# Where the Hyena filters are computed: both in expert passes 2 to 6 instead of at the head of each layer, with seven ring positions from the second lap on and the layer loop written out

## The chip, the cores and the metric

One Trainium2 chip, one core, float32 throughout. The time of a run is device microseconds of that core; fewer is better. The chip writes a float32 product as two matmul rows, so a count of matmul rows is twice the number of products in the code.

## The reference

Two blocks follow each other on x (256 tokens, 1024 features). The first has an mLSTM/gMLP mixer, a cross attention and a mixture of 32 experts. The second has two layers, each with three branches (Hyena convolution, gated linear attention, pooling), gates, and a feed-forward part. What the change touches is the Hyena filter, which depends on weights and positions alone and not on x:

```python
def _hyena_filter(t, z, w1, b1, fr1, w2, b2, fr2, w3):
    h = jnp.sin(fr1 * (z @ w1 + b1))
    h = jnp.sin(fr2 * (h @ w2 + b2))
    h = (h @ w3).astype(jnp.float32)
...
    decay = jnp.exp(-t * jnp.abs(deltas))
    h_fwd = h[:, :D_HYENA] * decay
    h_bwd = h[:, D_HYENA:] * decay
    return jnp.concatenate([h_fwd, zero, h_bwd[:0:-1]], axis=0)

def _hyena_mixer(u, conv_w, conv_b, t, z, w1, b1, fr1, w2, b2, fr2, w3, bias):
...
    k = _hyena_filter(t, z, w1, b1, fr1, w2, b2, fr2, w3)
    Zf = jnp.fft.rfft(zv, n=2 * L, axis=1)
    Kf = jnp.fft.rfft(k, n=2 * L, axis=0)
    y = jnp.fft.irfft(Zf * Kf[None], n=2 * L, axis=1)[:, :L]
...
    for i in range(DEPTH_2):
        h = _rms_norm(x, norm_mix_pre[i])
        proj = h @ w_in[i]
```

The transforms are products with cosine and sine tables.

## The kernel before

Each engine has its own program, written by hand, and runs the same list of regions in order: `first` (mixer, attention, routing), eight expert passes `pass0` to `pass7`, `extra` (a loop whose trip count is read on the chip: experts with more than 32 tokens get their further tokens here; with these inputs it runs once), `between` (final norm of the first block), `layers` (a hardware loop of two trips) and `last`. Engines meet on semaphores only. `Place.need` works out the count to wait for; inside the hardware loop it's a register's value plus a constant.

**Weights.** SP loads 2 MB blocks into ring positions: ten exist (`spots`), four as tensors of their own, six inside `zone`, where positions 0, 5, 6 and 9 also lie under tables and tiles of the layers. An expert pass computes four experts at once (32 tokens of each, side by side in the PE's columns) from 12 blocks: four for gate, four for up, four for down. Block k of all 96 goes to position k mod 10. `load` in `sp_prog` waits until the position's last user is done and issues the DMA. On PE, `slot` waits for the block; `release` only notes the position, and `first_mm` puts the signal `w_used` on the first product that comes behind and isn't alone in its group, or `flush` gives it at the end of the pass. The layers use a ring of four positions [7, 8, 3, 4] for 37 blocks a layer.

**A pass on PE** (`expert_pass`): tokens gathered by products (in0, in1), weights transposed, gate and up products, then `hid` transposed, down products, and products that scatter the result back (out). ACT and DVE evacuate between them. Blocks 0 to 9 are loaded ahead of pass 0.

**The head of a layer on PE** (`pe_layer`): transposes of the normed x (`norm_T`), f1 (filter, first product), hy0 (a block of the input projection, 32 products), f2, hy1, f3 (four products), hy2, then the four k groups (the filter's transform, ten products), then `lr`, q, gk, kk, zt and so on. DVE (`dve_layer`) takes each sine's argument to within pi in six instructions (`sine`), runs the three-tap convolutions of hy (`hconv`), multiplies f3 by the decay and forms sum and difference (hp_, hm_). ACT does the sines, the copies into `pad3`, and the copies of k into `Kf`. `zv`, the product of two convolved parts, is needed by the zt transposes behind kk.

**`between` on SP** waits for positions 0, 6 and 9 and loads the filter's weights, vec2, the whole table (2.9 MB), small2 and gate2 for layer 0; ACT loads the next layer's at each layer's end. `extra` loads three blocks into positions 1, 2 and 5, each when its position's last user is done.

Of the kernel before, what the change touches and what calls it, by code (L numbers as in the profile page):

```python
# [42 lines left out]
ZONE = 35200  # L43
# [11 lines left out]
EXPERT_RING = list(range(SPOTS))  # L55
EXTRA_RING = [1, 2, 5]
LAYER_RING = [7, 8, 3, 4]
PASS = [f"pass{i}" for i in range(PASSES)]

# [19 lines left out]
def _columns(table, parts):  # L79
    at = 0  # L80
    for name, n in parts:
# [14 lines left out]
_columns(TABLE, [("dft", 1024), ("sin0", 256), ("nyq", 128), ("inv", 1024), ("decay", 1024), ("band", 2048),  # L96
                 ("zT", 256)])
# [49 lines left out]
class Book:  # L147


    def __init__(self, counts):  # L150
        self.order = ["first"] + PASS + ["extra", "between", "layers", "last"]

        self.trips = {r: 1 for r in self.order} | {"extra": 0, "layers": NL}
# [7 lines left out]
class Banks:  # L161
# [46 lines left out]
    def all_taken(self, pl):  # L208
# [5 lines left out]
COUNTS = {'between': {'hs': 2,  # L214
             'ld_filt': 16,
             'ld_gate2': 16,
             'ld_small2': 16,
             'ld_table': 16,
             'ld_vec2': 16,
             'ms': 3,  # L220
             'pads': 1,
             'pool_step': 1,
             'rstd': 3,
             'sq': 4,
             'x_done': 2},
# [48 lines left out]
           'ld_const': 16,  # L274
           'ld_ident': 16,
# [3 lines left out]
           'ld_vec1': 16,  # L279
           'ld_x0': 16,  # L280
# [36 lines left out]
 'layers': {'Osq': 1,  # L317
# [5 lines left out]
            'filled0': 16,  # L323
            'filled1': 16,
            'filled2': 16,
            'filled3': 16,
            'filled4': 16,
            'filled5': 16,
            'filled6': 16,
            'filled7': 15,  # L330
            'filter': 1,
# [7 lines left out]
            'ld_filt': 16,  # L339
# [3 lines left out]
            'ld_vec2': 16,  # L343
# [6 lines left out]
            'sin': 2,  # L350
            'sinarg': 2,
            'sq': 12,
            'taken0': 16,
            'taken1': 16,
            'taken2': 16,
            'taken3': 16,
            'taken4': 16,
            'taken5': 16,
            'taken6': 16,
            'taken7': 15,  # L360
            'vector_step': 140,
# [12 lines left out]
            'zv': 1},  # L374
 'pass0': {'filled0': 2,
# [6 lines left out]
           'filled7': 1,  # L382
           'placed': 1,
# [9 lines left out]
           'w_ready0': 32,  # L393
           'w_ready1': 32,
           'w_ready2': 16,
# [7 lines left out]
           'w_used0': 2,  # L403
           'w_used1': 2,
           'w_used2': 1,
# [32 lines left out]
           'w_ready6': 16,  # L438
           'w_ready7': 16,
           'w_ready8': 16,  # L440
           'w_ready9': 16,
           'w_used0': 1,
           'w_used1': 1,
           'w_used2': 2,
# [2252 lines left out]
```

## Time and profile before

| what | value |
|---|---|
| runs (3) | 1986.69, 1986.70, 1989.63 us; median 1986.7 |
| profiled execution | 1987.02 us, its span 1984.8 us |
| mean granted TensorE clock | 0.932 of full |
| PE busy | 1754.0 us (88%), 7768 matmul rows |
| DVE, ACT, POOL busy | 467.6, 266.8, 23.4 us |
| DMA moved | 405.12 MB, mean 204 GB/s |
| first | 0 to about 330 us |
| passes 0 to 7 | about 330 to 770 us |
| extra and between | about 770 to 808 us |
| layer 0, layer 1 | 808 to 1391, 1391 to 1985 us |

Times of rows are us from the span's start. A busy share is an average over stages, so each stage is to be read by itself: which engine or transfer the others wait for there. "Idle before <-X" names what ended the wait; "issue" is a wait for nothing that the profile shows.

### The profile page before, as it was taken

How to read it: one execution, taken by the hardware profiler on the slowest of the kernel's cores; microseconds unless marked ns; L12 is line 12 of the kernel's file. 1: busy time of each engine (PE TensorE's matmuls, PEld its weight loads, DVE VectorE, ACT ScalarE, POOL GpSimd, SP SyncE). 2: the span in 40 equal slices, each digit the busy share in tenths (PEclk: the TensorE clock that was granted, in tenths of full speed). 3: DMA queues.
4: the chain of work that ended last, by engine and by line, in shares of the span. 5: the costliest groups of instructions: out<-in, count | busy, mean ns of one | idle time of the engine just before them, and what ended most of it. 6: DMA issues, size and time to landing. Idle time of an engine off the chain costs nothing.

```text
span 1984.8 us, 18851 instructions
## 1 busy us (share of the span) xinstructions
PE 1754.0 (88%) x7768; PEld 1164.0 (59%) x7768; DVE 467.6 (24%) x1005; ACT 266.8 (13%) x564; POOL 23.4 (1%) x46
## 2 busy tenths in 40 slices
PE   8999996766766667899999989999899999989998
PEld 7475654222221223676788568864676788578853
DVE  4223113311100111424321222211424322222211
ACT  2222121000000000213210010100113210010001
POOL 0010000000000000000000000000000000000000
PEclk9989997888777887899999989999899999989999
DMA  7432635999999999332233323361533133333260
GB/s 313 162 127 85 254 127 235 427 427 428 429 428 427 428 428 377 159 120 93 85 127 149 127 106 149 128 229 33 209 120 117 54 139 137 132 149 122 107 250 21
DMA packets 31781, 405.12 MB, mean 204 GB/s; under 512 B 3553, under 2 KB 4065, under 8 KB 7377
## 3 DMA queue, kind: packets, MB, share of 16 engines
q1 hardware_dynamic: 30608, 400.12, 50.2%
q10 hardware_dynamic: 1088, 3.78, 0.6%
q8 instruction: 64, 1.05, 0.2%
q14 instruction: 21, 0.16, 0.0%
HBM read 402.84 MB, written 1.05 MB: 203 GB/s over the span
## 4 chain that ended last, share of the span: by engine, by line
issue 60%; PE 22%; DMA 15%; DVE 2%; POOL 1%; ACT 1%; DVEq 0%; POOLq 0%; SPq 0%; ACTq 0%
PE bank L1016 22%; DMA zone<-in_w_experts 8%; DMA w<-in_w_experts 6%; PE bank L1060 1%; POOL stat L2547 1%; DVE zone L1890 0%; DMA x<-in_x 0%; DVE zone L1533 0%; DVE x L1940 0%; DVE zone L1773 0%; ACT zone L1356 0%; ACT zone L1348 0%; ACT zone L1374 0%; DVE x L1557 0%; DVE zone L1547 0%
## 5 line engine op out<-in xcount | busy, mean ns | idle before, releaser
L1016 PE MATMUL bank<-zone,w 128*128 128x256 f32 x3712 | 821.0, 384 | 4.4 <-DVE zone L1547 4.4
L1016 PEld LDWEIGHTS bank<-zone,w 128*128 128x128 f32 x3712 | 714.8, 193 | 112.2 <-issue 13.0
L1016 PE MATMUL bank<-w,zone 128*128 128x512 f32 (+1 forms) x1536 | 498.1, 659 | 64.5 <-DMA w<-in_w_experts 49.5
L1016 PE MATMUL bank<-zone 128*32 128x512 f32 (+9 forms) x2184 | 385.0, 532 | 89.4 <-DMA zone<-in_w_experts 62.4
L1016 PEld LDWEIGHTS bank<-w,zone 128*128 128x128 f32 (+1 forms) x1536 | 196.8, 164 | 347.6 <-issue 272.0
L1016 PEld LDWEIGHTS bank<-zone 128*128 128x128 f32 (+3 forms) x2184 | 205.2, 166 | 263.8 <-issue 154.6
L1374 ACT ACTIVATE zone<-bank 128x512 f32<-128x512 f32 (+2 forms) x136 | 77.5, 578 | 785.3 <-PE bank L1016 620.8
L1060 PE MATMUL bank<-const,zone 128*128 128x128 f32 (+2 forms) x286 | 47.6, 315 | 55.0 <-DVE zone L1533 34.5
L2341 DVE TENSOR_SCALAR zone<-zone,vec 128x256 f32<-128x256 f32 x68 | 28.0, 412 | 267.5 <-ACT zone L2199 267.5
L1060 PEld LDWEIGHTS bank<-const,zone 128*128 128x128 f32 (+2 forms) x286 | 38.3, 163 | 75.4 <-issue 30.7
L2199 ACT ACTIVATE zone<-bank 128x256 f32<-128x256 f32 x68 | 24.9, 384 | 360.0 <-PE bank L1016 360.0
L1888 DVE TENSOR_TENSOR zone<-zone,bank 128x512 f32<-128x512 f32 x8 | 5.5, 688 | 197.0 <-PE bank L1016 197.0
L2295 ACT ACTIVATE zone<-bank 128x512 f32<-128x512 f32 x16 | 9.6, 598 | 265.6 <-PE bank L1016 265.6
L2511 DVE TENSOR_TENSOR stat<-stat 128x1 f32<-128x1 f32 x8 | 1.3, 160 | 184.1 <-ACT zone L2295 184.1
L2547 POOL TENSOR_TENSOR stat<-stat 128x1 f32<-128x1 f32 (+2 forms) x29 | 17.3, 598 | 1924.4 <-DVE stat L1526 1924.4
L1890 DVE COPY zone<-bank 128x512 f32<-128x512 f32 x8 | 5.5, 692 | 143.3 <-PE bank L1016 143.3
L2494 DVE SCALAR_TENSOR_TENSOR zone<-zone,bank 128x256 f32<-128x256 f32 x16 | 6.8, 422 | 116.9 <-PE bank L1016 116.9
L2343 DVE SCALAR_TENSOR_TENSOR zone<-zone,vec 128x256 f32<-128x256 f32 x68 | 33.0, 485 | 2.4
L2342 DVE SCALAR_TENSOR_TENSOR zone<-zone,vec 128x256 f32<-128x256 f32 x68 | 33.0, 485 | 2.5
L1898 DVE TENSOR_TENSOR x<-bank,x 128x512 f32<-128x512 f32 x36 | 24.9, 692 | 17.7 <-PE bank L1016 17.7
L2476 DVE TENSOR_SCALAR zone<-bank 128x512 f32<-128x512 f32 x4 | 2.8, 692 | 79.3 <-PE bank L1016 79.3
L1016 PE MATMUL bank<-zone,const 4*128 4x256 f32 (+2 forms) x34 | 13.1, 550 | 8.6 <-DVE zone L1818 8.6
(228 smaller groups left out, 526.0 us busy)
## 6 DMA issues: line engine op xcount, KB each, us to landing
w<-in_w_layers SPq DMA_DIRECT2D x68, 2048.0 KB, 8.4
zone<-in_w_experts SPq DMA_DIRECT2D x61, 2048.0 KB, 42.1
w<-in_w_experts SPq DMA_DIRECT2D x38, 2048.0 KB, 42.1
w<-in_w_first SPq DMA_DIRECT2D x16, 2048.0 KB, 8.0
w<-in_w_layers SPq DMA_DIRECT2D x6, 1024.0 KB, 5.2
zone<-in_table SPq DMA_DIRECT2D x1, 2880.0 KB, 16.0
zone<-in_row ACTq DMA_DIRECT2D x2, 1024.0 KB, 4.8
const<-in_const SPq DMA_DIRECT2D x1, 1153.0 KB, 13.6
```

The source lines that it names most:

```text
L1016: return eng.matmul(out, lhsT, rhs, start=start, stop=stop, **kw_)
L1060: ins = eng.transpose(bank[0:m, at:at + n], src, idn)
L1374: A(dst, src, func, **k).then_inc(*banks.done(pl, name))
L1888: V.tensor_tensor(hid, sG, banks.tile(pl, "up"), ALU.mult).then_inc(*banks.done(pl, "up"))
L1898: V.tensor_tensor(xs, banks.tile(pl, f"out{t}{n}"), xs, ALU.add).then_inc(*banks.done(pl, f"out{t}{n}"))
L2199: return A(pad3[:, c % 3, 1:T + 1], bank[:, half * T:half * T + T], ACT.Copy)
L2295: A(ot[:, t, 512 * n:512 * n + 512], banks.tile(pl, name(t, n)), ACT.Square, accum_out=ssq[:, 4 + 2 * t + n:5 + 2 * t + n]).then_inc(*pl.u ...
L2341: v(pl, V.tensor_scalar(dst, src[:, 0:T], pv(VEC2, wname, 3 * c), pv(VEC2, bname, c), ALU.mult, ALU.add))
L2342: v(pl, V.scalar_tensor_tensor(dst, src[:, 1:T + 1], pv(VEC2, wname, 3 * c + 1), dst, ALU.mult, ALU.add))
L2343: V.scalar_tensor_tensor(dst, src[:, 2:T + 2], pv(VEC2, wname, 3 * c + 2), dst, ALU.mult, ALU.add).then_inc(*pl.up(signal))
L2494: w(V.scalar_tensor_tensor(m0, gates[:, c, :], 1.0, ba[:, 0:T], ALU.add, ALU.mult))
L2547: eng.tensor_tensor(rstd[:, col:col + n], ms[:, col:col + n], mhalf[:, 0:n], ALU.pow).then_inc(*pl.up(sem("rstd")))
```

## The change

It does five things. (1) f1, f2, f3 and k of both layers are computed in passes 2 to 6, between the up products and `hid`: f1 in pass 2, f2 in pass 3, f3 of layer 1 in pass 4, k of layer 1 and f3 of layer 0 in pass 5, k of layer 0 in pass 6. ACT's copies of k become DVE's. The results (`Kf`) stay in places of their own until the layers. (2) For tiles of the filter and for the first part of the table, positions 0, 5 and 6 are given up after their first use: from block 10 on the ring is [1, 2, 3, 4, 7, 8, 9]. (3) Loads move: the table is put in another order and its first 2432 of 5760 columns are loaded behind pass 0's blocks, with the filter's third matrices (64 partitions, 256 KB each); vec2 and the small filter matrices of both layers come in `first`; the rest of the table stays in `between`. (4) The layer loop is written out, and its waits are for constants. (5) The ring of the layers runs on from layer 0 to layer 1, where it began anew.

```diff
-EXPERT_RING = list(range(SPOTS))
+LATER_RING = [1, 2, 3, 4, 7, 8, 9]
+EXPERT_RING = list(range(SPOTS)) + [LATER_RING[i % len(LATER_RING)] for i in range(PASSES * ESLOTS - SPOTS)]
...
+        def filters(pl):
+            if pl.region == "pass2":
+                eng.wait_ge(*pl.need(sem("ld_filt"), 0))
+                eng.wait_ge(*pl.need(sem("ld_ftable"), 0))
+                for i in range(NL):
+                    group(pl, f"f1{i}", [((HFO, 0, T), [(w1f[i], tv("zT", HEMB))])])
+            elif pl.region == "pass3":
+                for i in range(NL):
+                    eng.wait_ge(*pl.need(sem("sin"), i + 1 - NL))
+                    group(pl, f"f2{i}", [((HFO, 0, T), [(w2f[i], h12[i])])])
+            elif pl.region == "pass4":
+                eng.wait_ge(*pl.need(sem("ld_filt3"), 0))
+                eng.wait_ge(*pl.need(sem("sin"), 0))
+                filter_out(pl, 1)
+            elif pl.region == "pass5":
+                eng.wait_ge(*pl.need(sem("filter"), 0))
+                filter_dft(pl, 1)
+                filter_out(pl, 0)
+            elif pl.region == "pass6":
+                eng.wait_ge(*pl.need(sem("filter"), 0))
+                filter_dft(pl, 0)
...
                 ins.then_inc(*banks.close(pl, kind))
+            filters(pl)
             for evacuated in banks.taken_up(pl, "up"):
...
-        group(pl, "f1", [((P, 0, T), [(w1f, tv("zT", HEMB))])])
...
-        tall(pl, "hy0", hT, 4)
-        eng.wait_ge(*pl.need(sem("sin"), 1))
-        group(pl, "f2", [((P, 0, T), [(w2f, h12)])])
-        tall(pl, "hy1", hT, 4)
-        eng.wait_ge(*pl.need(sem("sin"), 2))
-        for r in range(2):
-            for t in range(TT):
-                group(pl, f"f3{r}{t}", [((P, 0, 512), [(h12b[:, t * P:(t + 1) * P], w3f[:, 512 * r:512 * r + 512])])])
-        tall(pl, "hy2", hT, 4)
...
+        for i in range(3):
+            tall(pl, f"hy{i}", hT, 4)
...
+            eng.wait_ge(*pl.need(sem("w_used0"), 1))
+            eng.dma_start(table[:, 0:FILTER_TABLE], dram["table"][:, 0:FILTER_TABLE]).then_inc(*pl.up(sem("ld_ftable"), 16))
+            eng.wait_ge(*pl.need(sem("w_used6"), 1))
+            for layer in range(NL):
+                eng.dma_start(w3f[layer], dram["w_filt3"][layer]).then_inc(*pl.up(sem("ld_filt3"), 16))
...
         def between(pl):
-            for at in (0, 6, 9):
-                eng.wait_ge(*pl.need(sem(f"w_used{at}"), 0))
-            eng.dma_start(filt, dram["w_filt"][0]).then_inc(*pl.up(sem("ld_filt"), 16))
-            eng.dma_start(vec2, dram["vec2"][0]).then_inc(*pl.up(sem("ld_vec2"), 16))
-            eng.dma_start(table, dram["table"]).then_inc(*pl.up(sem("ld_table"), 16))
+            eng.wait_ge(*pl.need(sem("sin"), 0))
+            eng.wait_ge(*pl.need(sem("w_used9"), 0))
             eng.dma_start(small2, dram["w_small2"][0]).then_inc(*pl.up(sem("ld_small2"), 16))
             eng.dma_start(gate2, dram["w_gate2"][0]).then_inc(*pl.up(sem("ld_gate2"), 16))
+            eng.dma_start(table[:, FILTER_TABLE:], dram["table"][:, FILTER_TABLE:]).then_inc(*pl.up(sem("ld_table"), 16))
...
-                with eng.Fori(0, book.trips[region]) as it:
-                    parts[region](Place(book, region, it))
+                parts[region](Place(book, region))
```

On DVE the filter's steps (`sine`, `filter_sides`, `filter_kept`, the last with four copies of 128x512) stand behind the product of `hid` and ahead of the copy of down1; on ACT the sines of passes 2 and 3 stand between the copies of `hid` and of down0.

The head of a layer on PE. Before, from f3 to `lr` (16x256); bank<-zone,w 128x256 are the hy products, x10 the k groups, REGISTER_ALU the counts of the loop's waits:

```order
L1016 MATMUL bank<-zone 128x512 x2
L1045 REGISTER_ALU
L1016 MATMUL bank<-zone 128x512 x2
L1023 REGISTER_ALU
L1016 MATMUL bank<-zone,w 128x256 x16
L1045 REGISTER_ALU
L1016 MATMUL bank<-zone,w 128x256 x16
L2019 REGISTER_ALU
L1045 REGISTER_ALU
L1016 MATMUL bank<-zone 128x512 x10
L1045 REGISTER_ALU
L1016 MATMUL bank<-zone 16x256 x16
```

Of the change, from the transposes on, in either layer:

```order
L1069 MATMUL bank<-const,zone 128x128 x16
L1025 MATMUL bank<-zone,w 128x256 x96
L1025 MATMUL bank<-zone 16x256 x16
L1025 MATMUL bank<-zone,w 128x256 x32
L1025 MATMUL bank<-zone 128x256 x8
```

The three hy blocks (96 products) now stand together, `lr` right behind them.

Pass 5 on PE, from its last gate and up blocks to the next pass's gathers. Before (32x512 are expert products, 128x128 x4 the transposes of `hid`, 128x512 x4 out):

```order
L1016 MATMUL bank<-w,zone 32x512 x16
L1016 MATMUL bank<-zone 32x512 x16
L1016 MATMUL bank<-w,zone 32x512 x8
L1060 MATMUL bank<-const,zone 128x128 x4
L1016 MATMUL bank<-w,zone 32x512 x8
L1016 MATMUL bank<-zone 32x512 x24
L1016 MATMUL bank<-zone 128x512 x4
L1016 MATMUL bank<-zone 128x128 x16
```

Of the change:

```order
L1025 MATMUL bank<-w,zone 32x512 x32
L1025 MATMUL bank<-zone 32x512 x24
L1025 MATMUL bank<-zone 128x512 x14
L1069 MATMUL bank<-const,zone 128x128 x4
L1025 MATMUL bank<-w,zone 32x512 x32
L1025 MATMUL bank<-zone 128x512 x4
L1025 MATMUL bank<-zone 128x128 x16
```

Fourteen products of the filter (ten of k, four of f3) stand between up and `hid`.

SP at the end of pass 0. Before:

```order
L2588 DMA zone<-in_w_experts 128x4096 x2
L2588 DMA w<-in_w_experts 128x4096 x2
L2588 DMA zone<-in_w_experts 128x4096 x4
L2588 DMA w<-in_w_experts 128x4096 x2
L2588 DMA zone<-in_w_experts 128x4096 x2
```

Of the change:

```order
L2641 DMA w<-in_w_experts 128x4096 x2
L2641 DMA zone<-in_w_experts 128x4096 x3
L2689 DMA zone<-in_table 128x2432
L2692 DMA zone<-in_w_filt 64x1024 x2
L2641 DMA w<-in_w_experts 128x4096 x4
L2641 DMA zone<-in_w_experts 128x4096 x3
```

The part of the table and the two loads of filter weights go ahead of pass 1's first block.

## Rows read from the trace of the kernel before

**Rows 1.** The page's slices of 49.6 us each: DMA busy tenths, and GB/s.
```profile
DMA  7432635999999999332233323361533133333260
GB/s 313 162 127 85 254 127 235 427 427 428 429 428 427 428 428 377 159 120 93 85 127 149 127 106 149 128 229 33 209 120 117 54 139 137 132 149 122 107 250 21
```

**Rows 2.** Stretches of 20 us: busy us of each engine, PEclk, DMA share, GB/s.
```profile
440.00:460.00 20.00, 11.48 (x68) 2.57 (x68) 0.69 (x1) 0.60 (x1) 0.00 (x0) 0.83 1.00 424
1220.00:1240.00 20.00, 20.00 (x95) 17.60 (x94) 5.15 (x12) 2.06 (x6) 0.00 (x0) 1.00 0.31 130
```

**Rows 3.** PE timeline, passes 4 and 5: start, us, instruction, [idle before <-releaser].
```profile
583.17 3.64 PE L1016 MATMUL bank<-zone 128*32 128x512 f32 x16 [1.10 <-DMA zone<-in_w_experts]
...
596.72 5.36 PE L1016 MATMUL bank<-zone 128*32 128x512 f32 x48 [1.05 <-issue]
...
622.56 1.92 PE L1016 MATMUL bank<-w,zone 128*32 128x512 f32 x16 [1.38 <-DMA w<-in_w_experts]
...
627.55 3.17 PE L1016 MATMUL bank<-w,zone 128*32 128x512 f32 x16 [1.59 <-DMA w<-in_w_experts]
```

**Rows 4.** DMA issues, 330 to 770 us: count, KB, median us to landing.
```profile
zone<-in_w_experts SPq DMA_DIRECT2D x54, 2048.0 KB, 42.4
```

**Rows 5.** Five us at pass 0's start; columns as in rows 2.
```profile
330.00:335.00 5.00, 4.46 (x44) 1.76 (x48) 1.67 (x7) 0.00 (x0) 0.00 (x0) 1.00 0.21 46
```

**Rows 6.** PE's timeline, pass 0.
```profile
330.54 5.36 PE L1016 MATMUL bank<-zone 128*32 128x512 f32 x48 [1.12 <-issue]
...
342.55 1.93 PE L1016 MATMUL bank<-w,zone 128*32 128x512 f32 x16
```

**Rows 7.** DMA issues, whole span; columns as in rows 4.
```profile
w<-in_w_layers SPq DMA_DIRECT2D x68, 2048.0 KB, 8.4
...
zone<-in_table SPq DMA_DIRECT2D x1, 2880.0 KB, 16.0
```

**Rows 8.** PE's timeline, layer 0: hy1 and hy2, with f2 and f3 ahead.
```profile
824.60 0.70 PE L1016 MATMUL bank<-zone 64*128 64x256 f32 x2
825.23 14.08 PE L1016 MATMUL bank<-zone,w 128*128 128x256 f32 x64
839.24 3.70 PE L1016 MATMUL bank<-zone 64*128 64x512 f32 x8
842.87 14.08 PE L1016 MATMUL bank<-zone,w 128*128 128x256 f32 x64
```

**Rows 9.** PE by form, 808 to 870 us: count, busy us, mean ns, idle.
```profile
L1016 PE MATMUL bank<-zone 128*128 128x512 f32 x20 | 8.7, 592 | 0.0
```

**Rows 10.** PE's waits, 808 to 1400 us: us in total, times, longest.
```profile
PE bank L1016 <- DVE zone L2467: 0.2, 1, 0.2
```

**Rows 11.** Timeline from the leftover pass to layer 0's first product.
```profile
760.05 3.64 PE L1016 MATMUL bank<-zone 128*32 128x512 f32 x16 [1.25 <-DMA zone<-in_w_experts]
...
770.19 0.37 SPq L2640 DMA_DIRECT2D zone<-in_w_experts  x1
...
780.19 6.05 PE L1016 MATMUL bank<-zone 128*32 128x512 f32 x32
...
804.69 0.75 DVE L1533 TENSOR_SCALAR zone<-x,stat 128x1024 f32<-128x1024 f32 x1 [0.66 <-POOL stat L2547]
...
808.85 15.82 PE L1016 MATMUL bank<-zone,w 128*128 128x256 f32 x64
```

**Rows 12.** Timeline from layer 0's last products to layer 1's first.
```profile
1369.51 16.47 PE L1016 MATMUL bank<-w,zone 128*128 128x512 f32 x38
...
1391.39 3.05 PE L1060 MATMUL bank<-const,zone 128*128 128x128 f32 x12 [5.41 <-issue]
...
1392.52 0.75 DVE L1533 TENSOR_SCALAR zone<-x,stat 128x1024 f32<-128x1024 f32 x1 [0.66 <-POOL stat L2547]
...
1397.24 1.12 PE L1060 MATMUL bank<-const,zone 128*128 128x128 f32 x4 [2.80 <-issue]
...
1400.46 16.95 PE L1016 MATMUL bank<-zone,w 128*128 128x256 f32 x64 [0.96 <-DVE zone L1547]
```

More of the change, by code:

```diff
@@ L58 @@
 PASS = [f"pass{i}" for i in range(PASSES)]
+LAYER = [f"layer{i}" for i in range(NL)]
 def spot(ring, k, first=0):
@@ L150, in __init__ @@
     def __init__(self, counts):
-        self.order = ["first"] + PASS + ["extra", "between", "layers", "last"]
-        self.trips = {r: 1 for r in self.order} | {"extra": 0, "layers": NL}
+        self.order = ["first"] + PASS + ["extra", "between"] + LAYER + ["last"]
+        self.trips = {r: 1 for r in self.order} | {"extra": 0}
         self.counts = {r: counts.get(r, {}) for r in self.order}
@@ L1318, in extra, with layer @@
             eng.wait_ge(*pl.need(sem("extra_added"), 1))
-        run(eng, dict(first=first, extra=extra, layers=lambda pl: pe_layer(
-            pl, eng, group, transposes, norm_T, tall, wide, widest, slot, release, flush, mm, first_mm)) | {r: expert_pass for r in PASS})
+        def layer(pl):
+            pe_layer(pl, eng, group, transposes, norm_T, tall, wide, widest, slot, release, flush, mm, first_mm)
+        run(eng, dict(first=first, extra=extra) | {r: expert_pass for r in PASS} | {r: layer for r in LAYER})
     def run(eng, parts):
@@ L1510, in between, with layer @@
                 A(hs[:, t, :], x[:, t, :], ACT.Square, accum_out=ssq[:, t:t + 1]).then_inc(*pl.up(sem("sq")))
-        run(eng, dict(first=first, extra=extra, between=between,
-                      layers=lambda pl: act_layer(pl, eng, A, evac_T, copy, load_small2)) | {r: expert_pass for r in PASS})
+        def layer(pl):
+            act_layer(pl, eng, A, evac_T, copy, load_small2)
+        run(eng, dict(first=first, extra=extra, between=between) | {r: expert_pass for r in PASS} | {r: layer for r in LAYER})
     g8, e8, em, pen = lg[:, 80:96], lg[:, 96:112], lg[:, 112:176], lg[:, 176:184]
@@ L1942, in between, with layer @@
             scale_rows(pl, x, 4)
-        run(eng, dict(first=first, extra=extra, between=between,
-                      layers=lambda pl: dve_layer(pl, eng, V, v, ms_of, scale_tile, evac_T)) | {r: expert_pass for r in PASS})
+        def layer(pl):
+            dve_layer(pl, eng, V, v, ms_of, scale_tile, evac_T)
+        run(eng, dict(first=first, extra=extra, between=between) | {r: expert_pass for r in PASS} | {r: layer for r in LAYER})
     z = Zone(area, area + 4 * SLOT)
@@ L2573, in between, with layer @@
                 pw(pl, 2 + t, t, 1)
-        def layers(pl):
+        def layer(pl):
             for k in range(2 * TT * 2):
                 pw(pl, k + 1, (4 if k % 2 == 0 else 0) + k // 2 % TT, 1)
-        run(eng, dict(first=first, between=between, layers=layers))
+        run(eng, dict(first=first, between=between) | {r: layer for r in LAYER})
     def sp_prog(eng):
@@ L2660, in last @@
             eng.wait_ge(*pl.need(sem("stored"), 16))
[L2662 to L2667 removed]
+        run(eng, dict(first=first, extra=extra, between=between, last=last) | {r: expert_pass for r in PASS} | {r: layer for r in LAYER})
     with nc.Block() as block:
```

707 lines of the change are left out of this document (364 added, 343 removed).

## The prediction

> **What bounds the kernel now.** I read the page's slices first. From 350 to 750 us the DMA engines are full at 427 to 429 GB/s [rows 1]; before and behind they move a third of that. The 20 us tables say who works: from 440 to 460 us PE is busy 11.5 of 20 us at a mean granted clock of 0.83, with the DMA share at 1.00; from 1220 to 1240 us PE is busy all 20 us at clock 1.00 (2.4 GHz), with the DMA share at 0.31 [rows 2]. So there are two regimes: the expert passes are paid in bytes, the two layers in PE instructions. Then I read PE's timeline in a pass: PE waits for each block, and the last up block begins at 622.56 us, 39.39 us and eight blocks behind the last down block of the pass before: 4.92 us a block [rows 3], which is 2.1 MB at 427 GB/s. In the layers I read PE's timeline and its list of waits.
>
> **The filter's work in the layers (removed).** The chip writes a float32 product as two matmul rows. In layer 0, f2 holds PE from 824.60 to 825.23 (0.63 us), f3 from 839.24 to 842.87 (3.63 us) [rows 8], and the four k groups are 20 rows, 8.7 us [rows 9], of which the pipelining overlaps 0.1: 8.6 us. f1 stands before hy0, and hy0, at 808.85, waits for DVE's copy of the transposed norm anyway; f1 is hidden there and its removal gives nothing. Sum 12.86 us a layer, with no idle time of PE between the pieces, and 25.7 us for two. Does this reach the end? Between hy0 and the merging PE's list has one wait on another engine, 0.2 us on DVE [rows 10]. Everything that DVE and ACT do for later products (gates, decays, Y) hangs on products behind `lr`, and comes forward with them. The convolutions are fed by the hy products, 3.5 us of PE a chunk for three DVE instructions; only zv is older than `lr`, and it's needed behind q, gk and kk. DVE's six-step sines, its sums and ACT's copies and sines go too, all beside PE: 0 us. What is late next is nothing new: PE's own products. **-25.7 us.**
>
> **The written-out loop (moved).** At the turn from layer 0 to layer 1 PE ends its products at 1369.51 + 16.47 = 1385.98 us. The rows of token tile 0 have long been ready, but its transposes start only at 1391.39, after 5.41 us laid to "issue"; the last four of tile 1 stand again 2.80 us on "issue", and hy0 starts at 1400.46 [rows 12], 7.19 us behind the end of tile 1's scaling (1392.52 + 0.75). At the entry to layer 0, with no jump back, the same distance is 808.85 - (804.69 + 0.75) = 3.41 us [rows 11]. So 3.8 us of the turn belong to the jump. hy0 itself takes 16.95 us there and 15.82 at the entry, against 14.08 for a warm block [rows 8, 11, 12]: PE stood longer before it, and the clock came later; 1.1 us more. Bounds: 0 (stalls stay) and the 8.2 us of both stalls. I take **-4.9 us**, by the entry's row. The Trainium skill (Runtime: NRT & Kernel Launch, Instruction fetch mechanics) says that fetching ahead is purely sequential and a taken branch outside a two-page window stalls; by it the stalls are the jump's, and the sum would stand. The register arithmetic before the loop's waits shows no price: DVE's wait for POOL takes 0.66 us at the entry, where the counts are constants, and 0.66 in the loop [rows 11, 12]. 0 us.
>
> **The filter's work in passes 2 to 6 (added).** PE gets 2 groups of f1, 2 of f2, f3 in pass 4, four k groups and f3 in pass 5 and four k groups in pass 6, each between the last up product and `hid`. The most is pass 5: 14 products, 28 rows of 0.43 us, 12 us. They lie in time that PE would spend waiting for down blocks: before, up ends at 624.5 and the first down block starts at 627.55; now it starts near 640, with three blocks landed, which PE takes in 1.9 us each against 4.92 for the DMA, so by the fourth it has caught up. `hid` is queued behind the filter on PE, and ACT's and DVE's copies of `hid` and down behind that, all inside this time. DVE's ten instructions in pass 5 stand ahead of the copy of down1, which is due some 20 us later. 0 us, with the cover being the DMA's own 19.7 us for four blocks; without cover it would be 12 us.
>
> **Seven positions (changed).** A block's position is freed by the first product of the next block. So six blocks, 29.5 us, are queued when PE takes a block on landing; before it was nine, and 42.4 us from issue to landing says the same [rows 4]. The longest pause in freeing is at a pass's end: 583.17 to 596.72, 13.6 us, 2.8 blocks [rows 3]. In pass 5 the pause before down grows to 17 us, 3.5 blocks. Three blocks of cover remain at the worst. 0 us; the upper bound is in the rivals.
>
> **Bytes brought into the full stretch.** 2432 of the table's 5760 columns, 1216 of 2880 KB [rows 7], 2.9 us at 427 GB/s; w3 twice 256 KB, 1.2 us. Both queue on SP behind pass 0's last blocks; w3 waits for position 6, whose user's successor starts at 342.55, and SP's later loads with it. By then blocks 10 and 11 and the table, 12.7 us of DMA from about 336 on, keep the queue full [rows 5, 6]. w3 goes to 64 partitions; the Trainium skill (SBUF — State Buffer, Door 1) says that 64 reach half of the ports. By it w3 would take 2.4 us and the sum be 1.2 us worse; no row here shows a 64-partition load alone. Without the rule I bound w3 by 0 and, at the 377 GB/s of the slice with the small loads [rows 1], 1.4.
>
> **The first lap's end.** Block 10 waited for block 0's position and now waits for block 1's: three blocks take PE 5.36 us [rows 6], so the DMA, idle to about 334 (share 0.21) [rows 5], starts 1.7 us later, and being full from there on it never makes this up. Together **+5.8 us** on the end of pass 7; lower bound 2.9 (the table alone), upper 7 (SP held by w3 for one more block's products).
>
> **The stage between.** The leftover pass's second weight block used to be issued when block 92 was used; now position 2 holds block 95, freed at the flush, so it goes with the third at 770.19. It has 13 us until its product, behind the gate product of 780.19 [rows 11]; two blocks take 9.8 and some 3 of latency (8.4 us from issue to landing alone [rows 7]). 0 us, bounded by 3. Behind it stand small2, gate2, 1664 KB of table and hy0's weights: 8.1 MB from 770, 19 us and 3 of latency, to 793, against hy0 at 808.85: 0 us. The first stage loads 0.24 MB more, beside products: 0 us.
>
> **Sum.** -25.7 - 4.9 + 5.8 = -24.8 us on the profiled execution's 1987.0 us (span 1984.8 and 2.2 around it): 1962.2. Its time is 0.3 above the median of the runs, 1986.7, so the forecast is **1962 us**. A measurement of this kernel tells about 0.2%, 4 us, from no change.
>
> **Rivals.**
> Stalls in the passes. If PE's granted clock stays at its lower level through pass 5's filter (after a wait it often is: the block at 622.56 takes 1.92 us, that at 627.55 3.17 [rows 3]), 28 rows take 24 us, the pause reaches 30 us and eats all 29.5 us of queue; 4.9 us to refill once or twice, 5 to 10 us: 1967 to 1972. Against it: after a pause the first block of products (15.82 for 14.08) loses only 1.7 us [rows 8, 11]. Chance 0.11.
> The turn's stalls stay. If an engine pays for first-run code whether it jumps or not, -4.9 becomes 0: 1967. The Trainium skill's rule above speaks against it, and layer 0's entry shows no such stall. Chance 0.08.
> The queue runs dry in every pass (slower). Seven positions leave the DMA without work at each pass's end, in seven passes. It decides from 3.5 us a pass, which eats the 24.8; at one block, 4.9 us, in passes 1 to 7 it is 34 us: 1996. For it: 42 us of queue became 29.5. Against it: the pauses are 13.6 and 17. Chance 0.03.
> An engine takes PE's place in the layers (DVE with the decays), and most of the 12.86 us a layer comes back as waits, with +5.8 paid: about 1983 to 1988, no change. Against it: rows 10. Chance 0.02.
>
> **How the numbers follow.** The forecast has 0.76; its own unknowns (the turn between the bounds, w3 and the start of the queue, the clock between the passes and layer 0, some 2 us either way) give 1957 to 1967. The range goes up to 1970, to hold the stalled turn and the milder half of the stalled passes, and from 1957. Faster by over 0.2%: 0.76 + 0.11 + 0.08 = 0.95; within 0.2%: 0.02; slower: 0.03.
>
> **What would show it.** Right: the last down block of pass 7 begins some 5.8 us later (760.05 before [rows 11]), with DMA at 427 GB/s through and block spacing still 4.92; PE in hy0 to lr without a gap, lr 12.9 us nearer to hy0; no "issue" wait at the turn and layer 1's hy0 some 10.7 us behind layer 0's last product. Wrong: a slice of the passes under 420 GB/s; PE waits for `taken`, `filter` or `sin`; new "issue" waits in layer 1's code, or one on DVE between lr and gates.

## The result, and the profile after

| | before | changed |
|---|---|---|
| median of the runs shown with it | 1987.0 us (4) | 1952.7 us (4: 1951.2 to 1953.4) |
| ratio, 95% interval | | 0.9823, 0.9806 to 0.9840 |
| profiled execution, its span | 1987.0, 1984.8 us | 1952.2, 1950.3 us |
| mean granted TensorE clock | 0.932 | 0.941 |
| PE busy, matmul rows | 1754.0 us, 7768 | 1731.3 us, 7768 |

The time fell by 34 us. The forecast was 1962 with a range from 1957 to 1970: the sign was right, and the gain was 9.5 us larger than the sum of 24.8. Beside the experiments the kernel before was run 49 times more, in three sets; their medians are 1984.2 (21 runs), 1984.3 (11) and 1985.9 us (17), and single runs lie between 1977.2 and 1990.2. So one profiled execution set against another, as in the table below, carries a part that isn't the change's.

From the page of the changed kernel: the rows that answer to [rows 1], and the chain that ended last (shares of the span by engine):

```profile
DMA  7432544999999999733233324352333142333260
GB/s 316 173 130 87 226 162 154 402 430 430 429 429 430 429 430 387 287 129 121 87 130 151 130 86 173 130 225 108 141 118 130 49 167 109 157 145 133 84 237 22
...
PE 76%; DMA 19%; DVE 2%; issue 1%; ACT 1%; POOL 0%; DVEq 0%; POOLq 0%; SPq 0%; ACTq 0%
```

The DMA is full through the passes, at 429 to 430 GB/s where it had been 427 to 429, with one slice at 402 where the added loads lie. PE's timeline in pass 5, start, us, instruction, idle before:

```profile
627.27 3.64 PE L1025 MATMUL bank<-zone 128*32 128x512 f32 x16 [1.72 <-DMA zone<-in_w_experts]
632.12 16.52 PE L1025 MATMUL bank<-zone 128*32 128x512 f32 x44 [1.21 <-DMA zone<-in_w_experts]
648.57 0.66 PE L1069 MATMUL bank<-const,zone 128*128 128x128 f32 x4
650.12 7.07 PE L1025 MATMUL bank<-w,zone 128*32 128x512 f32 x64 [0.89 <-ACT zone L1421]
658.04 3.67 PE L1025 MATMUL bank<-zone 128*128 128x512 f32 x8 [0.85 <-issue]
```

The 44 rows are the last up block (16) and the 28 rows of the filter. They end at 648.6; then all four down blocks are there and go in 7.07 us without a wait. The filter lies in time in which PE would have waited. PE behind pass 7, at layer 0's head, around `lo` and at the turn:

```profile
763.62 3.27 PE L1025 MATMUL bank<-zone 128*32 128x512 f32 x16 [1.91 <-DMA zone<-in_w_experts]
768.46 1.92 PE L1025 MATMUL bank<-zone 128*32 128x512 f32 x16 [1.58 <-DMA zone<-in_w_experts]
771.29 3.67 PE L1025 MATMUL bank<-zone 128*128 128x512 f32 x8 [0.90 <-DVE zone L2000]
778.23 5.41 PE L1025 MATMUL bank<-zone 128*128 128x32 f32 x32 [3.26 <-DVE zone L2019]
...
784.23 4.92 PE L1025 MATMUL bank<-zone 128*32 128x512 f32 x32
...
811.70 41.68 PE L1025 MATMUL bank<-zone,w 128*128 128x256 f32 x192 [1.09 <-DVE zone L1600]
853.31 7.08 PE L1025 MATMUL bank<-zone 128*16 128x256 f32 x32
...
1101.07 7.13 PE L1025 MATMUL bank<-w,zone 128*128 128x512 f32 x16 [1.82 <-DVE zone L2557]
1109.56 20.87 PE L1025 MATMUL bank<-w,zone 128*128 128x512 f32 x48 [1.35 <-DMA w<-in_w_layers]
...
1371.12 1.07 PE L1069 MATMUL bank<-const,zone 128*128 128x128 f32 x8 [0.38 <-issue]
1378.16 1.97 PE L1069 MATMUL bank<-const,zone 128*128 128x128 f32 x8 [5.97 <-DVE zone L1586]
1381.22 43.15 PE L1025 MATMUL bank<-zone,w 128*128 128x256 f32 x192 [1.09 <-DVE zone L1600]
1424.29 7.08 PE L1025 MATMUL bank<-zone 128*16 128x256 f32 x32
```

From `hy0` (811.70) to `lr` (853.31) PE runs 192 rows without a gap. At the turn the "issue" waits of [rows 12] are gone: tile 0's transposes come 0.38 us behind the last product, tile 1's wait for DVE's scaling, as at the entry. Stretch by stretch in us, from these rows and those ahead; one execution of each kernel:

| stretch | before | changed | difference | predicted |
|---|---|---|---|---|
| start to pass 0's first gate product | 330.5 | 332.1 | +1.6 | 0 |
| from there to pass 7's last down block | 429.5 | 436.3 | +6.8 | +5.8 |
| from there to layer 0's hy0 | 48.8 | 43.2 | -5.6 | 0 |
| hy0 to `lr`, layer 0 | 56.6 | 41.6 | -15.0 | -12.9 |
| `lr` to the last product, layer 0 | 520.6 | 517.4 | -3.2 | 0 |
| turn, last product to hy0 | 14.5 | 10.5 | -4.0 | -3.8 |
| hy0 to `lr`, layer 1 | 57.7 | 43.1 | -14.6 | -12.9, -1.1 |
| `lr` to the end of the span | 526.6 | 526.0 | -0.6 | 0 |

### The profile page after: what moved, and what is told of

It reads as the page before. It is cut to its first block, busy times and chain, and to the rows that moved or that the text cites. A ratio compares the mean times of both kernels' runs of the same rounds, so it can differ in the third digit from the quotient of the medians.

```text
span 1950.3 us, 17947 instructions
## 1 busy us (share of the span) xinstructions
PE 1731.3 (89%) x7768; PEld 1160.9 (60%) x7768; DVE 473.3 (24%) x1013; ACT 256.8 (13%) x552; POOL 23.5 (1%) x46
## 4 chain that ended last, share of the span: by engine, by line
PE 76%; DMA 19%; DVE 2%; issue 1%; ACT 1%; POOL 0%; DVEq 0%; POOLq 0%; SPq 0%; ACTq 0%
PE bank L1025 74%; DMA w<-in_w_experts 10%; DMA zone<-in_w_experts 9%; PE bank L1069 1%; DMA w<-in_w_layers 1%; POOL stat L2600 0%; DVE zone L1586 0%; DMA x<-in_x 0%; DVE zone L2568 0%; DVE x L2573 0%; ACT zone L1412 0%; DVE zone L1600 0%; ACT zone L2384 0%; ACT zone L2387 0%; DVE x L2050 0%
## 5 line engine op out<-in xcount | busy, mean ns | idle before, releaser
L1025 PE MATMUL bank<-w,zone 128*128 128x512 f32 (+1 forms) x1760 | 523.6, 653 | 75.7 <-DMA w<-in_w_experts 58.7
L1025 PEld LDWEIGHTS bank<-w,zone 128*128 128x128 f32 (+1 forms) x1760 | 203.8, 157 | 374.7 <-issue 287.5
L1025 PE MATMUL bank<-zone 128*32 128x512 f32 (+10 forms) x1960 | 339.3, 488 | 70.7 <-DMA zone<-in_w_experts 47.1
L1025 PEld LDWEIGHTS bank<-zone 128*128 128x128 f32 (+3 forms) x1960 | 194.7, 167 | 218.1 <-issue 132.4
L1421 ACT ACTIVATE zone<-bank 128x512 f32<-128x512 f32 (+1 forms) x128 | 72.7, 577 | 768.8 <-PE bank L1025 580.4
L1069 PE MATMUL bank<-const,zone 128*128 128x128 f32 (+2 forms) x286 | 46.9, 312 | 49.6 <-DVE zone L1586 41.0
L2295 ACT ACTIVATE zone<-bank 128x256 f32<-128x256 f32 x68 | 24.8, 384 | 358.6 <-PE bank L1025 358.6
(226 smaller groups left out, 526.6 us busy)
```

The costliest lines, as they stand in the source:

```text
L1025: return eng.matmul(out, lhsT, rhs, start=start, stop=stop, **kw_)
L1069: ins = eng.transpose(bank[0:m, at:at + n], src, idn)
L1421: A(dst, src, func, **k).then_inc(*banks.done(pl, name))
L2295: return A(pad3[:, c % 3, 1:T + 1], bank[:, half * T:half * T + T], ACT.Copy)
```

## Experiments

Twelve kernels ran. Each diff shows only the lines that carry the edit. The changed kernel itself has the four runs above and one profile; where a number here is set against its 1952.7 us, the runs come from different sets, whose medians of the kernel before lie within 1.8 us of each other. Where a stretch is counted from the "first transfer", that is the moment in pass 0 at which the DMA, idle till then, begins again, taken from windows of 1 us (334.5 us in before, 337.5 in the changed kernel), so good to some 0.3 us.

**1. The loop alone.**

```diff
-        self.order = ["first"] + PASS + ["extra", "between", "layers", "last"]
+        self.order = ["first"] + PASS + ["extra", "between"] + LAYER + ["last"]
```

> The kernel before with the layer loop alone written out (filters stay at the head of each layer, ten positions, the layers' ring begins anew in layer 1). Nothing ahead of 808.85 us (layer 0's hy0) may move. By the prediction's step: the turn from layer 0's last product (1385.98) to layer 1's hy0 (1400.46) falls from 14.5 to about 10.7 us, hy0 of layer 1 from 16.95 to 15.8: -4.9 us, 1982.1. Theory A (the extra gain of the change is the granted clock's, not the loop's): the same, between -4 and -5. Theory B (the register arithmetic ahead of the loop's waits has a price on the path): in addition some 1 to 1.5 us in each layer between lr and the last product, the wait of lo for its block shorter by 0.8 us in both: -6.5 to -8, 1979 to 1980.5.

Measured: 1973.3 us median (6), ratio 0.9953 (0.9935 to 0.9970), 6 to 13 us below before, where the prediction's step gave 4.9. PE's timeline of this kernel at the turn:

```profile
1375.86 1.07 PE L1119 MATMUL bank<-const,zone 128*128 128x128 f32 x8 [0.38 <-issue]
1382.90 1.97 PE L1119 MATMUL bank<-const,zone 128*128 128x128 f32 x8 [5.98 <-DVE zone L1592]
...
1385.96 6.38 PE L1075 MATMUL bank<-zone,w 128*128 128x256 f32 x20
```

Its DMA issues, columns as in [rows 4]:

```profile
w<-in_w_layers SPq DMA_DIRECT2D x68, 2048.0 KB, 7.7
```

The turn is 10.5 us, as in the change. In both layers the wait on DVE of [rows 10] is gone, the wait of `lo` for its block is 1.8 and 1.5 us (2.2 and 2.1 before), and a block lands 7.7 us behind its issue where it took 8.4 [rows 7]. Together these are some 1.2 us a layer that the prediction had at 0. But this kernel also differs ahead of 808.85, where nothing had been edited. PE at the head of layer 0:

```profile
803.78 14.05 PE L1075 MATMUL bank<-zone,w 128*128 128x256 f32 x64 [0.46 <-DVE zone L1606]
817.76 0.70 PE L1075 MATMUL bank<-zone 64*128 64x256 f32 x2
...
836.02 14.08 PE L1075 MATMUL bank<-zone,w 128*128 128x256 f32 x64
849.94 15.76 PE L1075 MATMUL bank<-zone 128*128 128x512 f32 x52
```

hy0 begins 5 us earlier and takes 14.05 for 15.82 us: the same instructions at another granted clock. With hy0 at the full clock, hy0 to `lr` is 849.94 + 8.7 - 803.78 = 54.8 us, against 41.6 without the filter: 13.2 us a layer.

**2. Seven positions alone.**

```diff
-EXPERT_RING = list(range(SPOTS))
+EXPERT_RING = list(range(SPOTS)) + [LATER_RING[i % len(LATER_RING)] for i in range(PASSES * ESLOTS - SPOTS)]
```

> The kernel before with seven ring positions from block 10 on, and nothing else. By the prediction: the last down block of pass 7 begins 1.7 us later (761.75 for 760.05), DMA at 427 GB/s through, no pause of DMA at any pass's end: 1988.7. Theory A (what PE's granted clock does at the end of pass 7 depends on where in time the blocks fall): the same 1.7 us, and then up to 5.5 us either way in the leftover pass: 1983 to 1990. Rival (seven positions starve the queue): each pass longer by up to 4.9 us, 2000 and more.

Measured: 1985.1 us (10), ratio 1.0016 (0.9996 to 1.0035). From pass 0's first gate product (333.17) to the last down block (764.50) 431.3 us, 1.8 more than before. DMA stays at 427.9 GB/s. The prediction's 1.7 holds, and the rival in which the queue runs dry is refuted.

**3 and 4. Without the filter's work, and also without its loads.** Both leave the filter's result out: the Hyena branch works with transforms set to zero.

```diff
-            filters(pl)
```
```diff
-            eng.dma_start(table[:, 0:FILTER_TABLE], dram["table"][:, 0:FILTER_TABLE]).then_inc(*pl.up(sem("ld_ftable"), 16))
-            eng.wait_ge(*pl.need(sem("w_used6"), 1))
-            for layer in range(NL):
-                eng.dma_start(w3f[layer], dram["w_filt3"][layer]).then_inc(*pl.up(sem("ld_filt3"), 16))
```

> The changed kernel without the filter's products, sines, sums and copies in passes 2 to 6 (the kept transforms are set to zero, so the Hyena branch's output is not computed from a filter; the loads stay). If the filter's work in the passes is wholly hidden, as the prediction has it, the last down block of pass 7 begins at 768.5 as in the changed kernel and the time is 1952.7 within 2 us. If it cost the passes anything: earlier by that, the prediction left 1.0 us of the passes unexplained. Theory C (the filter's products hold PE's granted clock up through the passes, and the 5.5 us between pass 7's last block and hy0 are theirs): without them this stretch is back at about 48.8 us, for 43.2, 1958.

> The changed kernel without the filter's work in the passes (the kept transforms are set to zero) and without the two loads behind pass 0's blocks (the table's first part, w3): the bytes brought into the full stretch, taken away alone. Runs so far, from pass 0's first gate product to pass 7's last down block: before 429.5 us, seven positions alone 431.3, change without filter work 436.4, the change 436.3. By the prediction's terms the bytes are 2.9 + 1.2 = 4.1 us: 432.3 here. By a load on 64 partitions at half speed 5.3: 431.1. Rival: the filter's or the loads' place in SP's queue (SP held by w3's wait) costs the rest: then above 431.3 by that. Time: about 5 us less than the change without filter work, 1947.

Measured: 1951.7 us (4) without the work, 1948.9 (6) without work and loads. Work: pass 0's gate to the last down block is 436.4 us against 436.3, so it is hidden, and theory C is refuted (pass 7's last block to hy0 is 46.3 us here, within what kernels with the filter's work show, 43.2 to 46.3). Loads: from the first transfer to the last down block 431.0 us with them, 423.5 without. That is 7.5 us for what was put at 4.1, and 423.5 is 2.1 less than the 425.6 of before. Two terms were off, in opposite directions. Stretches of 5 us of the changed kernel, columns as in [rows 2]:

```profile
350.00:355.00 5.00, 5.00 (x52) 1.73 (x44) 0.00 (x0) 0.29 (x1) 0.00 (x0) 1.00 1.11 270
355.00:360.00 5.00, 4.10 (x16) 1.44 (x8) 2.77 (x4) 0.30 (x1) 0.00 (x0) 1.00 0.96 343
```

The same of number 4, without the loads:

```profile
350.00:355.00 5.00, 5.00 (x52) 1.89 (x48) 0.00 (x0) 0.00 (x0) 0.00 (x0) 1.00 1.01 433
355.00:360.00 5.00, 4.11 (x22) 1.56 (x15) 1.81 (x3) 0.60 (x1) 0.00 (x0) 1.00 1.02 436
```

The DMA engines count as busy but move 270 and 343 GB/s where the small loads lie.

**5. Before, begun later.**

```diff
+            V.memset(kx.rearrange("p k t -> p (k t)"), 0.0)
+            V.memset(vx.rearrange("p t d -> p (t d)"), 0.0)
             scale_rows(pl, x, 2)
```

> The kernel before with two memsets of 128x2048 on DVE ahead of the first normalization, in tensors that are written later anyway: everything starts some 2 to 4 us later, no other work moves. Theory A (PE's granted clock after a wait depends on when in the run the wait falls): the delay d seen at the first product does not come out as 1987.0 + d, stretches behind waits (the gate rows near 136, the routing at 304 to 330, the stretch from pass 7's last block to hy0, 48.8 us) become longer or shorter by some tenths to 5 us, each without any change of work. Rival (the clock follows only from the order of work and waits, which is the same): each stretch as before within 0.3 us, and the time 1987.0 + d.

Measured: 1988.1 us (10), ratio 1.0007 (0.9990 to 1.0025). Pass 7's last block to hy0 took 46.5 us for 48.8, hy0 14.05 for 15.82, the turn 13.9 for 14.5. That speaks for theory A, but the 21 runs of the unchanged kernel beside it, spread over 13 us, say more: the clock that is granted behind a wait differs from one execution to the next. Over the profiled kernels this stretch took 48.8, 43.6, 45.2, 46.5 and 48.3 us with before's code (the last is number 9's), and 43.2, 46.3, 46.2, 46.3, 43.3 and 46.1 with the changed kernel's. Before's own profile was an unlucky one: the longest of its five.

**6. Each layer in a loop of one trip, and 7. the registers in its waits.**

```diff
+                with eng.Fori(0, 1) as it:
+                    parts[region](Place(book, region, it))
```
```diff
+                one = eng.value_load(xtab[0:1, 3 * XN:3 * XN + 1], min_val=0, max_val=XN)
+                parts[region](Place(book, region, one))
...
+            return sig.sem, (self.it + (base + n - 1) if base + n > 1 else base + n)
```

> The changed kernel with each layer in a hardware loop of one trip: the waits count by registers again (the arithmetic ahead of each wait is back), the code of either layer is still its own and no jump back is taken at the turn. Theory A (the registers' arithmetic is what the layers lost behind lr, 2.4 to 2.8 us a layer between the transposes of v's block and the last product; the jump is what the turn lost): both layers' stretches back from 477.2 and 476.7 to about 479 to 480, a wait of some 0.2 us on DVE in the gated attention, the waits at the merging and of lo longer by 0.1 and 0.3 to 0.7; the turn stays at 10.5 us: 1957. Rival 1 (the arithmetic is free, the layers' stretches follow the granted clock or the ring that runs on from layer to layer): no change, 1952.7. Rival 2 (it is entering a loop, not jumping back, that stalls the engines at the turn): the turn back to 14 us as well, 1960.

> The changed kernel, its layers still written out and without a loop, where every wait in them is for a register plus a constant, the register being a value read once per layer and engine (the count of the leftover pass's trips, 1 with these inputs). This puts the arithmetic ahead of the waits back, which a loop of one trip did not do. Theory A (the arithmetic is what the layers lost behind lr): the stretches from the transposes behind v's block's predecessor to the last product back from 477.2 and 476.7 to about 479, with a wait of 0.2 us on DVE in the gated attention and the DVE rows of the gates spaced by 0.19 for 0.10 us: about 1957. Rival (the loop's code, not its arithmetic, or the granted clock): stretches as they are within 0.5 us, 1952.7.

In number 6 the loop's counts came out as constants (DVE's steps in the gates stand 0.10 us apart, as in the change, not 0.19 as before), so it tested the loop's entry and exit alone: 1955.6 us (5), the turn at 10.5 us, the layers' stretches as in the change. No stall shows at the turn, where one loop ends and the next is entered. Its profiled span is 2.2 us longer, and the stretch behind pass 7 alone is 3.0 us longer (46.3 for 43.2), most of it in products at the lower clock. Yet its five runs (1954.5 to 1956.8) all lie above the changed kernel's four (1951.2 to 1953.4), so a cost of 1 to 3 us elsewhere isn't excluded. The Trainium skill (Runtime: NRT & Kernel Launch, Instruction fetch mechanics), which the prediction cited, says that a taken branch to outside the two fetched pages stalls, and the turn agrees: 13.9 to 14.5 us in the four kernels with the jump back, 10.5 without it. Number 7 has the arithmetic: 1953.2 us (5). DVE's timeline of number 7 in a gate shows its price:

```profile
1078.28 0.42 DVE L2560 TENSOR_TENSOR zone<-zone 128x256 f32<-128x256 f32 x1 [0.19 <-DVE zone L2556]
```

The stretches between the transposes behind `kk` and the last product are 477.4 and 476.8 us, against 477.2 and 476.7. Theory A is refuted: the arithmetic lengthens a dependent wait from 0.10 to 0.19 us and costs about 0.3 us a layer on PE's path, which shorter waits elsewhere cancel. The block's landing stays at 7.5 us with registers in SP's waits, and was 8.3 to 8.5 in each kernel with the loop of two trips, where the addresses come from a register as well. So the slower landing belongs to that loop; that the register address is its cause is a guess, which wasn't tried alone.

**8. w3 on 128 partitions.**

```diff
-    w3f = [spots[6][0:HFO, 2048:3072], spots[6][0:HFO, 3072:4096]]
+    w3f = [spots[6][:, 2048:2560], spots[6][:, 2560:3072]]
```

> The changed kernel with the filter's third matrices loaded on 128 partitions (two times 128x512, 256 KB as before) for 64 partitions of 1024; the second sine is also written to partitions 64 to 127, and f3's right half is taken from there. The runs show that the DMA moves 170 to 250 GB/s for 5 us where these loads lie, and that all bytes brought into the full stretch cost 7.5 us (431.0 from the first transfer to pass 7's last down block, 423.5 without them), of which the table's 1216 KB are 2.9. Theory D (the 64 partitions keep the DMA engines from sharing these loads evenly, 4.6 us for 512 KB): this stretch 427.7 to 428.5, no dip in GB/s, the time 3 us less, 1949.5. Rival (small loads cost that anyway, or SP's wait for position 6 does): 430.5 to 431, no change.

Measured: 1950.4 us (5: 1950.1 to 1952.8). From the first transfer to the last down block 427.6 us, 3.4 less (3.1 less if counted from pass 0's first gate product, 433.3 for 436.3), and the dip is gone. Its stretches of 5 us:

```profile
350.00:355.00 5.00, 4.14 (x40) 1.26 (x32) 0.69 (x1) 0.60 (x1) 0.00 (x0) 1.00 1.07 447
355.00:360.00 5.00, 4.70 (x17) 2.50 (x18) 2.76 (x4) 0.00 (x0) 0.00 (x0) 1.00 0.99 423
```

So two loads of 256 KB on 64 partitions cost 1.2 + 3.1 to 3.4, 4.3 to 4.6 us, in a full queue; numbers 3 and 4 give 7.5 - 2.9 = 4.6. The Trainium skill (SBUF — State Buffer, Door 1) says that 64 partitions reach half of the ports; the direction agrees, but the cost by it is an estimate of 2.4 us, which is less than the runs show. The edit also halves the bytes of a partition in each load, 4 KB to 2 KB, so what makes these loads so dear isn't separated.

**9. The address of the zone.**

```diff
+    sb("moved", VEC2["all"][1])
     zone = sb("zone", ZONE)
```

> The kernel before with an unused tensor of 173 columns ahead of the zone, so that the zone and the six ring positions in it begin at the byte address that they have in the changed kernel; nothing else is changed. DMA moves 427.8 GB/s from 362 to 755 us in the four runs with the old address and 430.0 in the five with the new one, and blocks into the zone come 4.84 us apart in place of 4.90. Theory E (the address of the ring's positions sets this): 430.0 GB/s, the last down block of pass 7 2.1 us nearer to the first transfer (423.5 for 425.7), the time 2 us less than before. Rival (it is the seven positions with the other order of places, or where the inputs lie in memory): 427.8 and no change.

Measured: 1983.9 us (12), ratio 0.9993 (0.9981 to 1.0005), so the time alone can't tell. The stretch can: from the first transfer to the last down block 423.3 for 425.6 us. The stretch from 400 to 740 us of before (columns as in [rows 2]):

```profile
400.00:740.00 340.00, 222.38 (x1376) 71.55 (x1376) 37.41 (x85) 17.00 (x41) 0.00 (x0) 0.83 1.01 428
```

The same of number 9:

```profile
400.00:740.00 340.00, 225.73 (x1384) 72.42 (x1376) 37.37 (x85) 17.01 (x41) 0.00 (x0) 0.83 1.01 431
```

An unused tensor of 692 bytes a partition ahead of the zone makes the weights' stream 0.6% faster. Number 9 has one profile, but the groups are clear: 428 GB/s in these 340 us in all four profiles with the old address, 430 or 431 in all with the new one. The change did this by accident, as vec2 became twice as wide and lies ahead of the zone.

**10, 11, 12. Products of constants in PE's waits.** They write a bank that is free and nobody reads; number 10 has them behind pass 7 and in the layers, number 11 in the first stage too, number 12 adds number 8's edit.

```diff
+            for i in range(n):
+                mm(banks.tiles[b], ident, const[:, 0:512], i == 0, i == n - 1)
```

> The changed kernel with products of constants (128x512, result never read) on PE where it waits: 3 behind pass 7, 8 ahead of layer 0's transposes, 6 between the two tiles' transposes at the turn, and 6 between those ahead of each feed-forward. They add 0.86 us each at the higher clock, all inside waits of 3.3, 9.0, 6.0 and 6.5 us, if the clock is at the higher level when they begin. Theory A (PE stands at the lower level behind a wait and pays for it, by luck of the run): the transposes behind the waits take 0.96 for 1.97 us (1.9 for 3.67 at layer 0's entry), layer 1's hy block 41.6 for 43.1, the leftover pass's gathers 3.8 for 5.4 and its gate and up 3.6 for 4.9, and the run to run spread shrinks: about 8 us less, 1944. Rival (these products do not hold the clock up, or they overrun the waits at the lower level): no change or up to 5 us more.

> The same, and in the first stage 4 products ahead of the transposes of the gate rows (wait of 3.9 us), 2 between the two tiles' transposes of two normalizations, 4 ahead of the ranks (wait of 8.6 us). Theory A: the stretch 136 to 150 shorter by 1 to 2 us, the block behind the second normalization 27.8 for 29.9, the gathers of pass 0 faster, pass 0's first gate product at about 328 for 332: 3 to 4 us below the kernel with the fillers behind pass 7 alone, 1941. Rival: the fillers begin at the lower clock and overrun, no gain or a loss of up to 3 us.

> The changed kernel with products of constants in PE's waits in the first stage, behind pass 7, at the head of the layers and ahead of the feed-forward, and the third matrices on 128 partitions. If the two gains (1952.7 to 1942.1 and about 3 us) are independent: 1939. If the fillers' gain was luck of the runs: 1946 to 1950.

Measured: 1945.7 (5), 1942.1 (6) and 1937.3 us (5), ratios to before 0.9808, 0.9788 and 0.9763 (0.9746 to 0.9779): number 12 beats both kernels, the changed one by 15 us, and the gains of 10 and of 2 to 3 us add. PE's timeline of number 10:

```profile
776.27 2.84 PE L1025 MATMUL bank<-const 128*128 128x512 f32 x6
779.43 3.76 PE L1025 MATMUL bank<-zone 128*128 128x32 f32 x32 [0.32 <-DVE zone L2034]
...
783.78 3.64 PE L1025 MATMUL bank<-zone 128*32 128x512 f32 x32 [0.34 <-DVE zone L2038]
...
790.66 2.76 PE L1025 MATMUL bank<-zone 128*32 128x512 f32 x16 [1.34 <-DMA zone<-in_w_experts]
...
1130.67 5.32 PE L1025 MATMUL bank<-const 128*128 128x512 f32 x12
1137.38 1.09 PE L1069 MATMUL bank<-const,zone 128*128 128x128 f32 x8 [1.39 <-DVE zone L1601]
```

The transposes ahead of the feed-forward take 1.09 for 1.97 us, and its 704 rows 153.9 and 152.2 for 154.4 and 153.9. The gathers behind pass 7 take 3.76 for 5.41 here, but 4.96 and 4.58 in numbers 11 and 12, whose gate and up still take 5.39 and 5.79: short products of constants hold the clock up often, not always. What is late next in number 10 is the leftover pass's third block (1.34 us on the DMA). The spread of the runs did not shrink as expected: 5.9, 10.2 and 6.3 us, against 2.2 in four runs of the changed kernel. That the gain is the clock's shows in the rows that got shorter; how much of the 7 to 11 us each filled wait gives wasn't taken apart.

## Why the prediction was right or wrong

The step that failed is the pricing of TensorE's clock. The forecast allowed "the clock between the passes and layer 0, some 2 us either way", read from one execution; the terms of work, loop and bytes add up to -26.3 us by the runs where the sum had -24.8, which alone would have stayed in the range, and the other 5 to 7 us lie in stretches whose instructions are unchanged. Term by term:

**Filter out of the layers, -25.7: right, a little small.** 13.2 us a layer at the full clock (number 1 against the change) for 12.86. The rest of the 15.0 and the 14.6 us is the clock of hy0 in the one profile of before: its first 64 rows took 1.8 us less afterwards in layer 0, 1.5 us less in layer 1.

**The loop, -4.9: too small a term, and one of its steps wrong.** The turn gave 4.0 us (3.4 to 4.0 against the four profiles with the loop of two trips) for 3.8. The 1.1 us for hy0's clock at the turn seem to have come (1.5 us in this pair of profiles), but by luck. PE at layer 1's hy0, number 2 with the turn's stalls, then number 7 without them:

```profile
1396.14 15.49 PE L975 MATMUL bank<-zone,w 128*128 128x256 f32 x64 [0.40 <-DVE zone L1506]
```
```profile
1380.29 44.71 PE L1027 MATMUL bank<-zone,w 128*128 128x256 f32 x192 [1.06 <-DVE zone L1605]
```

Counted to the next block's start, hy0 takes 15.4 us in number 2, with the stalls, and 16.9 in number 7, without them (its 44.71 us hold two more blocks of 13.9). Over the profiles either code shows both values, so the stall doesn't set them. "The register arithmetic shows no price: 0 us" was right in its number; but what stood behind it, that the loop costs nothing within a layer, was wrong: 1.2 us a layer, from blocks that land 0.8 us later and from waits on DVE, and 0.3 us outside the span (2.2 before, 1.9 after). Number 1's 9.3 us (6 to 13) is 4.0 + 2.4 + 0.3; the rest is put down to the clock, of which the profiles show a part: in layer 0 `lo` took PE 22.5 us in three of the four profiles with the loop of two trips, behind waits of 2.2 to 2.3 us, and 20.9 in the fourth, behind 0.7, and in all ten others, behind 1.3 to 1.8.

**Filter in passes 2 to 6, 0: right**, number 3 shows it. Its rival (stalled passes) did not occur; the filter's rows in passes 4 to 6 ran at the full clock.

**Bytes and the first lap, +5.8: right in sum, from two wrong sizes.** The first lap's end is 1.8 (1.7 predicted). The bytes are 7.5 for 4.1, since w3 costs 4.3 to 4.6 for 1.2; its bound, 0 to 1.4, was taken from the rate of a slice that holds both full stream and small loads [rows 1], and this term was mis-sized by a factor of almost four. The address of the zone gives 2.1 to 2.3 back, which no step looked at. 1.8 + 7.5 - 2.2 = 7.1 against the 6.8 measured.

**The stage between and the first stage, 0: right** as to work. The +1.6 and most of the -5.6 us of the two profiles are the clock behind waits: pass 0's first gate product lay at 330.5 to 333.2 with before's code and at 330.7 to 333.3 with the changed.

**The sum.** -26.4 (filter), -4.0 (turn), -2.4 (loop within the layers), -0.3 (outside), +6.8 (passes) are -26.3 us, where -24.8 was forecast. From 1984.2 to 1985.9, the medians of many runs, to 1952.7 it is 31.5 to 33.2 us. Of the 5 to 7 that are left, means over the profiles of either code lay some 1.3 us in the stretch behind pass 7, 1.2 in `lo` of layer 0 (1.6 in three of four), 1.0 in the two layers' hy0, and 1.1 in layer 1's feed-forward (704 rows from the first one's start to the next row's: 154.7 to 155.0 with the loop of two trips, 153.5 to 153.7 with the changed kernel's code). The instructions are the same in each, so this is clock. These are means of four to six profiles, so the split is argued and not shown; why the changed code is granted more clock stays open. The rest, 1 to 2 us, is within what four runs of one kernel can tell. Two numbers fit this reading: the lowest run of before, 1977.2 of over fifty, and the lowest of the changed kernel's four, 1951.2, are 26.0 us apart, about what the terms of work give. The forecast thus gave "some 2 us either way" to a quantity that moves before's own time over 13 us, and it started from 1986.7, up to 2.5 us above the medians of the later sets.

## What to carry to other kernels

Where work leaves an engine that waits for nobody, the gain is its rows' time, and that could be read in advance to 3%; what could not is the TensorE clock behind each wait, so run the kernel before some twenty times ahead of a forecast, start from their median, and give the range at least their spread. In a queue that is full, don't price a small load on 64 partitions by its bytes alone: here it cost almost four times as much. When a table ahead of a large buffer changes its width, measure the transfer rate into the buffer.

## What the runs showed of the hardware

- The granted TensorE clock behind the same wait differs between executions of one program: the leftover pass's gate and up took PE 4.6 to 6.3 us, hy0 in layer 0 14.05 to 15.8 us, and before's whole time was 1977 to 1990 us.
- It also falls without a wait. The 64 rows of `kk`, which stand behind 16 rows of 16 partitions, take 14.08 us in 7 of 28 cases (14 profiles, two layers), 15.8 in 19, and 16.7 and 17.1 in layer 0 of numbers 11 and 12. Of before, three stretches (columns as in [rows 2]):

```profile
886.00:890.00 4.00, 4.00 (x19) 3.03 (x17) 0.00 (x0) 2.90 (x7) 0.00 (x0) 1.00 0.40 94
890.00:893.00 3.00, 3.00 (x10) 2.33 (x10) 2.36 (x2) 1.05 (x3) 0.00 (x0) 0.65 1.00 423
893.00:896.00 3.00, 3.00 (x12) 2.53 (x11) 0.00 (x0) 0.00 (x0) 0.00 (x0) 0.78 0.38 158
```

  PE is busy all the time, and the granted clock is 0.65 and 0.78 of 2.4 GHz in the mean over 6 us, so 1.2 GHz for part of them. That the 16 rows are the cause isn't shown.
- Two loads of 256 KB on 64 partitions slow the full stream to 270 and 343 GB/s in two stretches of 5 us, with the engines counted as busy: 4.3 to 4.6 us for 0.5 MB.
- The stream into the ring moves at 428 GB/s or 430 to 431; in number 9 the address at which the zone begins is all that was changed.
- Blocks of the layers land 7.5 to 7.7 us behind their issue in written-out code, 8.3 to 8.5 in the loop of two trips.
